# A two-layer diffusion and flow-matching backbone on 8 cores: output weights first in their slot, modulation blocks later, last products of several chunks, squares added in pairs

## The reference

```python
def trunk(x, cond, s_in_f, s_in_b, rows):
    for l in range(DEPTH):                       # 2 layers
        mod = (jax.nn.silu(cond) @ ada_w[l] + ada_b[l])[:, None, :]
        sh_m, sc_m, g_m, sh_f, sc_f, g_f = jnp.split(mod, N_MOD, axis=-1)
        h = rmsnorm(x, norm_mix_g[l]) * (1.0 + sc_m) + sh_m
        y = even_mixer(h, ...) if l % 2 == 0 else odd_mixer(h, ...)
        x = x + g_m * y
        h = rmsnorm(x, norm_ffn_g[l]) * (1.0 + sc_f) + sh_f
        x = x + g_f * (jnp.square(jax.nn.relu(h @ ffn_w1[l])) @ ffn_w2[l])
    return rmsnorm(x, final_norm_g), ...

def even_mixer(h, w_in, w_out, ..., norm_g, s0_f, s0_b):
    q, k, v, g, lr_f, lr_b, fin = _split(h @ w_in, EV_SIZES)
    ...                                          # log decays from lr_f and lr_b
    o, s_f, s_b = gla_bidir(q, k, v, la_f, la_b, s0_f, s0_b)    # 4 heads, both directions
    o = o * lax.rsqrt(jnp.mean(o * o, axis=-1, keepdims=True) + EPS) * norm_g
    o = o.reshape(bsz, L, GLA_DV) * jax.nn.silu(g)
    fo = jnp.fft.fftn(fg, axes=(1, 3), norm='ortho').real
    return jnp.concatenate([o, fo], axis=-1) @ w_out, s_f, s_b
```

## Time and profile before

| | us |
|---|---|
| median of 3 runs | 1104.89 (1104.58 to 1105.58) |
| the profiled execution | 1108.39 |
| its span on its slowest core, which is the one shown | 1107.3 |
| spans of the 8 cores in it | 1100.5 to 1107.3 |
| TensorE busy | 1065.3 (96%) |
| VectorE busy | 611.7 (55%) |
| ScalarE busy | 428.8 (39%) |
| GpSimd busy | 165.2 (15%) |

### The profile page before, as it was taken

How to read it: one execution, slowest core, us unless ns; L and a number is a source line. 1 busy time by engine, 2 the same in 40 slices (tenths; PEclk the granted TensorE clock), 3 DMA queues, 4 the chain that set the end, 5 groups by cost and what they waited for, 6 DMA issues and landing times.

```text
span 1107.3 us, 15395 instructions; the slowest of 8 cores (1100.5 to 1107.3 us)
## 1 busy us (share of the span) xinstructions
PE 1065.3 (96%) x6012; PEld 534.3 (48%) x6012; DVE 611.7 (55%) x1118; ACT 428.8 (39%) x825; POOL 165.2 (15%) x203
## 2 busy tenths in 40 slices
PE   3699999899999999999999999999999999999997
PEld 0356877654444444444444444444444444444445
DVE  5343899966667686878224638567572222222228
ACT  5266899756743000233105611347632001332023
POOL 5001443324100000000104100044000000000021
PEclk9999999999999999999999999999999999999999
DMA  9998872429626856754921221442342142142106
GB/s 220 178 197 131 140 157 52 128 77 204 110 48 105 132 96 104 125 84 70 152 48 29 39 46 31 76 76 49 67 76 48 29 76 48 29 76 48 29 1 228
DMA packets 17737, 101.32 MB, mean 91 GB/s; under 512 B 1898, under 2 KB 7178, under 8 KB 11136
## 3 DMA queue, kind: packets, MB, share of 16 engines
q0 software_dynamic: 9584, 81.07, 42.9%
q1 hardware_dynamic: 7536, 18.87, 5.3%
q10 hardware_dynamic: 544, 0.39, 0.1%
HBM read 166.98 MB, written 7.86 MB: 158 GB/s over the span
## 4 chain that ended last, share of the span: by engine, by line
PE 89%; DVE 4%; DMA 3%; ACT 2%; POOL 1%; issue 1%; ACTq 0%; DVEq 0%; POOLq 0%
PE psf L324 89%; DMA sb_slot<-adaP 3%; DVE sb_X L345 2%; ACT sb_A L339 1%; POOL sb_X L115 0%; PE psf L1175 0%; POOL sb_slot L115 0%; DVE sb_A L345 0%; DVE sb_B L345 0%; DVE sb_A L342 0%; ACT sb_B L339 0%; DVE sb_att L342 0%; ACT sb_X L353 0%; DVE sb_X L342 0%; PE psf L1307 0%
## 5 line engine op out<-in xcount | busy, mean ns | idle before, releaser
L324 PE MATMUL psf<-sb_hT,sb_slot 128*128 128x512 bf16 x2472 | 551.9, 382 | 0.0
L324 PEld LDWEIGHTS psf<-sb_hT,sb_slot 128*128 128x128 bf16 x2472 | 241.3, 98 | 286.7 <-issue 16.2
L324 PE MATMUL psf<-sb_A,sb_slot 128*128 128x512 bf16 (+2 forms) x1696 | 359.5, 371 | 0.0
L324 PEld LDWEIGHTS psf<-sb_A,sb_slot 128*128 128x128 bf16 x1696 | 165.1, 98 | 188.1 <-issue 1.2
L339 ACT ACTIVATE sb_relu<-psf 128x512 bf16<-128x512 f32 x192 | 114.1, 595 | 354.3 <-PE psf L324 353.1
L345 DVE SCALAR_TENSOR_TENSOR sb_X<-psf,sb_modT,sb_X 128x512 f32<-128x512 f32 (+2 forms) x148 | 108.4, 734 | 217.1 <-PE psf L324 216.9
L342 DVE TENSOR_TENSOR sb_A<-sb_relu 128x512 bf16<-128x512 bf16 x192 | 81.5, 425 | 141.4 <-ACT sb_relu L339 141.0
L339 ACT ACTIVATE sb_B<-sb_X 128x512 bf16<-128x512 f32 (+2 forms) x96 | 55.7, 607 | 163.2 <-DVE sb_X L345 145.8
L324 PE MATMUL psf<-sb_slot,sb_hT 128*128 128x192 bf16 (+1 forms) x576 | 79.7, 290 | 0.6 <-ACT sb_X L353 0.2
L566 POOL TENSOR_TENSOR sb_B<-sb_B 128x512 f32<-128x512 bf16 (+2 forms) x48 | 59.3, 1242 | 121.2 <-ACT sb_B L339 120.6
L781 DVE SCALAR_TENSOR_TENSOR sb_B<-sb_slot,sb_B 128x1024 bf16<-128x1024 bf16 x56 | 68.3, 1219 | 0.4
(11 more groups left out here) (143 smaller groups left out, 691.0 us busy)
## 6 DMA issues: line engine op xcount, KB each, us to landing
sb_slot<-w POOLq DMA_DIRECT2D x16, 2048.0 KB, 16.2
sb_slot<-adaw POOLq DMA_DIRECT2D x14, 1024.0 KB, 10.8
sb_slot<-adaw POOLq DMA_DIRECT2D x3, 2048.0 KB, 20.2
sb_X<-xT SPq DMA_DIRECT2D x6, 1024.0 KB, 10.3
sb_X<-xT POOLq DMA_DIRECT2D x8, 512.0 KB, 11.2
sb_slot<-adaP POOLq DMA_DIRECT2D x8, 512.0 KB, 29.5
yT<-sb_X SPq DMA_DIRECT2D x8, 512.0 KB, 2.9
sb_X<-xT POOLq DMA_DIRECT2D x2, 1024.0 KB, 48.0
```

The lines of the kernel that those rows point to most:

```text
L324: T.op("pe", lambda: nc.tensor.matmul(out, l, r, start=start, stop=stop), reads=R, writes=W, sig=stop if sig is None else sig)
```

## The change

1. Order of the weights. `evO` is now the first load into slot 0 and stays there. The three modulation blocks go through slot 1, after `evH01`, and `dft` comes into slot 1 after them.
2. `ada_block` runs at the end of steps 13, 16 and 19 in place of 1, 6 and 11, and `evO_scale` in steps 0 to 5 in place of 16 to 21.
3. The deferral in `outproj` becomes 7, 5 and 3 groups for blocks 2, 0 and 1 (before: 5, 5 and 3).
4. In `final_parts` the gain is multiplied in by ACT (`gscale`), and the product with the root becomes a tensor product over several chunks at once: 4 and 4 chunks for the first part, 4, 2 and 2 for the last, each with one store. In the second part one of these is issued behind a group and not two.
5. The squares of block 1 at the start are added in pairs on DVE, and `x1_stat` has four matmuls in place of eight.

```diff
@@ order of the weights
         wadd("evH01", 2 * 8 * 448, evH_d[0])
-        wada(0, 2)
+        wadd("evO", 8192, evO_d)
         wadd("evH23", 2 * 8 * 448 + 1024, evH_d[1])
-        wada(0, 3)
+        for b in range(2, 5):
+            wada(0, b)
         wadd("dft", 8192, dft_d)
-        wada(0, 4)
-        wadd("evO", 8192, evO_d)
-        early = (1, 0, 2, 0, 1, 0, 0)
+        early = (1, 0, 2, 1, 1, 1, 1)
@@ outproj
+                lag = {MO[0]: 7, MO[1]: 5, MO[2]: 3}[m]
...
-                stat4(m, oc, 3 if m == MO[2] else 5)
+                stat4(m, oc, lag)
...
-                    pe_defer(3 if m == MO[2] else 5, lambda: norm_end(m, nxt))
+                    pe_defer(lag, lambda: norm_end(m, nxt))
@@ final_parts
-                def ap(c):
-                    stt(xT[m][:, c, hs], xT[m][:, c, hs], pp[:, PP_GFIN + c:PP_GFIN + c + 1], ntm[1][:, hs], ALU.mult, ALU.mult,
-                        [st["r"], pp_b], [xh[c]])
-                    if c % 2 == 1:
-                        T.dma("act" if q and c % 4 == 1 else "sp", y_d[m, :, c - 1:c + 1, hs], xT[m][:, c - 1:c + 1, hs], yo_b,
-                              reads=[xh[c - 1], xh[c]])
+                def ap(c0, n):
+                    xs = xT[m][:, c0:c0 + n, hs]
+                    tt(xs, xs, ntm[1][:, hs].unsqueeze(1).to_broadcast([128, n, hs.stop - hs.start]), ALU.mult, [st["r"]], xh[c0:c0 + n])
+                    T.dma("act" if q and c0 == 4 else "sp", y_d[m, :, c0:c0 + n, hs], xs, yo_b, reads=xh[c0:c0 + n])
 
                 rs_()
-                side.extend([lambda c=c: ap(c) for c in range(8)])
+                side.extend([lambda e=e: ap(*e) for e in (((0, 4), (4, 2), (6, 2)) if q else ((0, 4), (4, 4)))])
...
+            def gscale(c, hs, xb):
+                act(xT[m][:, c, hs], xT[m][:, c, hs], AF.Identity, [pp_b], [xb], scale=pp[:, PP_GFIN + c:PP_GFIN + c + 1])
...
-                    side_pop(3 - hh)
+                    gscale(oc, hs, xh[oc])
+                    if hh == 0:
+                        gscale(o, slice(0, 320), xhs[0][o])
+                        gscale(o, slice(320, 512), xhs[1][o])
+                    side_pop(3 - 2 * hh)
@@ squares of block 1
+            for c in range(lo, lo + 4, 2):
+                tt(sqr["t"][c], sqr["t"][c], sqr["t"][c + 1], ALU.add, [sqr["b"][c + 1]], [sqr["b"][c]])
...
-            for c in range(8):
-                mm(sbank[1][0][:], onesb[:], sqr["t"][c], [sqr["b"][c], on_b], [sbank[1][1]], start=(c == 0), stop=(c == 7), sig=True)
+            for c in range(0, 8, 2):
+                mm(sbank[1][0][:], onesb[:], sqr["t"][c], [sqr["b"][c], on_b], [sbank[1][1]], start=(c == 0), stop=(c == 6), sig=True)
@@ the pipeline of the even mixer
-            if 16 <= it < 22:
-                evO_scale(it - 16)
+            if it < 6:
+                evO_scale(it)
...
-            if it in (1, 6, 11):
-                ada_block(0, 2 + it // 5)
+            if it in (13, 16, 19):
+                ada_block(0, it // 3 - 2)
```

## The result

| | us |
|---|---|
| before, median of 5 | 1105.58 |
| changed, median | 1118.7 |
| ratio | 1.0114 (95% interval 1.0102 to 1.0126) |
| its profiled execution, span on its slowest core | 1116.0 |
| spans of its 8 cores | 1110.8 to 1116.0 |

The account below looks back on a forecast made before the run. PE, busy for 1065.3 of 1107.3 us, was taken as the bound. The terms 11.4 - 0.4 - 1.0 - 0.1 + 0.5 = +10.4 us on 1104.9 gave 1115.3 us, with an 80% range of 1110 to 1120 us.

Parts of the forecast that it names:

- The first wait: End of step 13: PE waits 7.4 us (7.0 to 8.5) for the first modulation block's weights, a 16.2 us load.
- a sign of being wrong: Modulation weight loads (`adaw`) under 14 us, or a wait under 4 us at the first block, would show the forecast wrong.
- The second wait: End of step 16: PE waits 3.1 us (1.6 to 3.1) for the second modulation block's weights, a 17.3 us load.
- The third wait: End of step 19: PE waits 2.7 us (2.3 to 3.8) for the third modulation block's weights, a 16.2 us load.
- the gaps in steps 14 to 19 that no longer count: PE's gaps of 0.96 and 0.88 us cost nothing while a load decides the next block's start: -1.8 us.
- The output weights early: Scaling leaves steps 20 to 23, closing half of PE's 0.80 us of gaps there: -0.4 us (0 to -0.8).
- the deferral: Output projection: two more groups of matmuls cover PE's 1.03 us wait for POOL's sum of squares: -1.0 us (0 to -1.0).
- The rival in the prediction: Waiting halves PE's clock after the first block; if the slow stretch lasts longer, some 1.5 us more: 1116.8 us, chance 0.10.
- Squares in pairs: At the start, four products with ones save 0.9 us, but DVE's additions come late: -0.1 us (-0.9 to +0.3).
- The end: Last products: 0.8 us less on DVE, but the last residual addition 1.4 us late, then stores: +0.5 us (-0.7 to +1.3).
- The second term: Stores at the end: DMA engines already full, and 768 KB become ready within one microsecond instead of 2.7.
- The base: The profiled execution (span 1107.3 us) is 3.5 us slower than the runs' median; the sum was put on 1104.9 us.

Follow-up runs that it names:

- e6: e1 with 26 unread products of 512 columns put on PE ahead of the first modulation block; 1.0119, +13 us against the kernel before.
- e3: The kernel before with only the deferral of 7 groups for block 2 in the output projections; 0.999, -1.1 us.
- e10: The kernel before with only the last products over several chunks and large stores, final gain left out (measurement only); 1.0015.
- e7: The kernel before with the final gain on ACT, but products with the root chunk by chunk and stores in pairs of chunks; 1.0012, +1.3 us.
- e5: e1 with the modulation blocks at the end of steps 15, 19 and 23, not 13, 16 and 19; 1.0013, +1.4 us against the kernel before.
- e1: The kernel before with only the changed weight order, modulation blocks at steps 13, 16 and 19, and scaling in steps 0 to 5; 1.0104, +11.5 us.

## Why the prediction was right, point by point

**The time.** 1115.3 was forecast, in a range of 1110 to 1120; it is 1118.7, the ratio 1.0114 where the forecast was 1.0094, +12.6 us for +10.4. The cause is the one forecast: loads of 16 us that are wanted too early. Of the three waits two came as forecast. The second did not, and two terms were too small, the clock behind the third wait and the end.

**The first wait** (7.4 us, 7.0 to 8.5): 7.47 on the slowest core. The load took 16.2 us as assumed. On the four cores with faster loads, 5.4 to 6.0; I had not thought of cores that differ. Single loads there took 13.7 to 13.9 us, under the 14 us that I had named as a sign of being wrong, and the forecast held because the slowest core sets the time.

**The second wait** (3.1 us) did not come: 0 to 0.5. I had said that the slow clock would be paid out of it, and so it was, 2.2 us of it; the other 0.9 is the load, which took 16.3 and not 17.3 us. Cores 0 and 5 of e6 show it: with the clock up, a wait of 2.3 and 2.5 us is there.

**The third wait** (2.7 us): 2.42. Together with the gaps in steps 14 to 19 that no longer count, steps 0 to 19 lost 10.6 us (core 7 against core 7), and the forecast was 11.4.

**The output weights early and the deferral** (-0.4 and -1.0 us): both right alone. In e3 the deferral gave 1.1; on cores 1 and 2 of the changed kernel the stretch from step 20 on is 89.7 us, 1.6 under that of before. On the six others the clock leaves 0.2 us of it at most, and on core 4 it takes more than that.

**The clock.** Here a step failed. The rival in the prediction was that the slow stretch behind the first wait lasts longer than what the second wait absorbs. On the slow cores it did not; but I had priced the clock behind the first wait alone and put nothing for the third. Behind the third wait (2.42 us, and then the block's 64 small products) PE of core 4 ran at 0.51 of its clock for 5.8 us, and nothing absorbed that: step 20 took 7.8 us where cores 1 and 2, whose clock stayed up, took 5.0. That is +2.8 us on core 4, +1.5 on core 7 and +1.7 on four others.

**Squares in pairs** (-0.1 us): 3.90 us against 3.89. Right, with its reason: the products wait for the additions.

**The end** (+0.5 us, -0.7 to +1.3): +2.2 to +2.5 us, outside the bounds. The durations on DVE were right (the products of 1280 columns took 1.49 us, forecast 1.43; the last ones 1.90, forecast 1.88), though the 1.05 ns a column behind them do not follow from the three rows named, which between 192 and 512 columns give 0.89. The main term missed was ACT. I let its products with the gain delay the root of the first part by 0.3 us and nothing else; there are three of them per group in the part of 320 columns, 1.36 us in groups of 2.3 us that have a square, and at one place a root, to do as well. So the squares came late, PE waited for them (2.7 us at the end, before 1.0), the first long product began 1.7 us late, and the last addition was 2.7 us late, not 1.4. In e10, without the gains, the first long product begins when it did before, and DVE is done when it was. The second term was the stores: I gave them 0.2 us, and the last one lands 0.8 us later behind DVE. e7 gives 1.4 us for the gains, e10 0.7 for the stores.

**The base.** The span of before that I started from had 6 us of low granted clock in it, but I had put the sum on the median, and that was right. The loads that I had looked at were not all: in the same trace the first load of a modulation block in the mixer took 20.2 us, two other weight loads took 15.5 and 15.7, and the tables, 2 MB too but without a change of type, 14.9. So 15.8 us was not the least, by little, and 17.3 not the most.

## What to carry to other kernels

When loads are moved to another slot, write down for each the moment at which its slot is free, the time of such a load on the slowest core, and the moment of use; every load behind it in the slot moves too, and in e5 the last of the row was the one that hurt. Where PE is the bound, an idle time ahead of little work can cost twice, by itself and by the clock behind it (on six of the eight cores here), unless another wait stands behind that takes it up. And an operation that is moved to an idle engine is free only if it does not stand ahead of one on the path: ACT was busy for 39% of the span, and its additional operations cost 1.4 us.

## What I had not expected of the hardware

- The cores of one chip differ in the time of the same load in the same execution: 13.7 to 15.0 us on four of them and 15.2 to 16.3 on the other four, in the changed kernel; which cores these are changes from chip to chip or run to run (in e1 cores 1, 2 and 7 have it fast, in the changed kernel 0, 3, 5 and 6).
- The load of the Fourier tables, which puts 2 MB into SBUF without a change of type, from the queue of SP, took 9.4 us on core 4 and 7.3 to 8.7 on the others, where the modulation weights, 2 MB in SBUF from 4 MB of float32, from the queue of POOL, took 13.7 to 16.3. (The Trainium skill, page "DMA: Bandwidth & Descriptors", section "Anatomy of one DMA — SWDGE (gpsimd) path", gives 2.0 us and the bytes at 436 GB/s, an estimate of 11.6 us for the 4 MB read. The trace does not agree: the fastest of these loads in the changed kernel took 13.7 us, and the fastest in any run 12.5, on core 4 of e6.) The row of the tables' load on core 4:

```profile
sb_slot<-dft SPq DMA_DIRECT2D x1, 2048.0 KB, 9.4
```

- A wait of 0.56 us and 64 products of two columns behind it were enough for the granted clock to fall to half (changed kernel, core 3); after waits of 2.00 and 2.31 us, on cores 1 and 2, it did not fall. The length of the wait alone does not decide it, and these runs do not tell what does.
